# Accumulating the weighted sum of squares of a double RMS norm on VectorE instead of TensorE

## The reference, cut to what matters

```python
def rms_norm(x, g):
    xf = x.astype(jnp.float32)
    y = xf * lax.rsqrt(jnp.mean(xf * xf, axis=-1, keepdims=True) + EPS)
    return (y * g.astype(jnp.float32)).astype(x.dtype)

# end of the first block
    x = x + peer_layer(rms_norm(x, norm_ffn_g), w_peer_q, peer_keys, peer_u, peer_v)
    return rms_norm(x, norm_final_g)
# start of the second block (x is what the first one returned)
        h = rms_norm_2(x, norm_g[l]) * (1.0 + scl[:, None, :]) + shift[:, None, :]
        proj = h @ w_in[l]
```

## Time and profile before

| | |
|---|---|
| median of three runs | 2390.09 us (2389.08 to 2395.07) |
| profiled execution, its own time | 2384.56 us |
| its span, first to last instruction | 2382.8 us |
| TensorE matmul busy over the span | 2057.4 us (86%) |
| VectorE busy | 1554.3 us (65%) |
| ScalarE busy | 479.9 us (20%) |
| GpSimd busy | 835.0 us (35%) |
| mean granted TensorE clock | 0.921 of full speed |

### The profile page before, as it was taken

One profiled execution on the slowest core, in us unless ns is written; L12 is line 12 of the kernel. 1 busy time (PEld: TensorE's weight loads), 2 busy tenths in 40 slices (PEclk: granted clock), 3 DMA queues, 4 the chain that ended last, 5 costly groups with the idle time before them and its releaser, 6 DMA issues. The chain is left out here.

```text
span 2382.8 us, 24401 instructions
## 1 busy us (share of the span) xinstructions
PE 2057.4 (86%) x8044; PEld 1367.7 (57%) x8044; DVE 1554.3 (65%) x3438; ACT 479.9 (20%) x1077; POOL 835.0 (35%) x633
## 2 busy tenths in 40 slices
PE   5998789969798989989889889988866679989977
PEld 4875468748547966555555555555422367724445
DVE  4468746459999956666666666666777676246752
ACT  3344122222212320000000000000000131335541
POOL 3420034423110026655555445454676222300002
PEclk8988589979899989999999999999988789999999
DMA  7976879667473679999999999999999421100012
GB/s 282 347 288 203 300 287 390 237 259 264 169 280 118 212 287 396 404 403 402 402 402 402 403 404 402 402 402 403 402 399 401 188 94 62 53 22 1 1 36 70
DMA packets 203900, 648.09 MB, mean 272 GB/s; under 512 B 19840, under 2 KB 52736, under 8 KB 202496
## 3 DMA queue, kind: packets, MB, share of 16 engines
q1 hardware_dynamic: 118384, 335.60, 37.9%
q0 software_dynamic: 73728, 268.47, 28.6%
q10 hardware_dynamic: 11664, 42.47, 5.2%
HBM read 560.48 MB, written 85.98 MB: 271 GB/s over the span
## 5 line engine op out<-in xcount | busy, mean ns | idle before, releaser
L1591 PE MATMUL ps<-arena 128*128 128x512 f32 x1024 | 519.2, 655 | 144.6 <-DVE arena L1448 92.5
L1459 DVE CUSTOM_DVE_ANT_0 arena<-arena 128x1024 bf16<-128x1024 f32 x256 | 313.3, 1224 | 246.4 <-DMA arena<-u_rows,u_row 132.8
L1580 PE MATMUL ps<-rows_n,arena 128*128 128x256 f32 x2048 | 464.7, 379 | 0.0
L1580 PEld LDWEIGHTS ps<-rows_n,arena 128*128 128x128 f32 x2048 | 387.0, 190 | 96.3 <-issue 50.4
L1591 PEld LDWEIGHTS ps<-arena 128*128 128x128 f32 x1024 | 207.9, 209 | 399.5 <-issue 269.1
L1323 POOL DMA_INDIRECT arena<-u_rows,u_row x256 | 290.7, 1136 | 313.2 <-DMA gates<-arena 168.5
L1323 POOL DMA_INDIRECT arena<-in_v,expert x192 | 209.3, 1090 | 315.9 <-DVE arena L1480 288.2
L1480 DVE SCALAR_TENSOR_TENSOR arena<-arena,wt 128x1024 f32<-128x1024 f32 x192 | 246.1, 1282 | 0.5
L1557 ACT ACTIVATE ge<-dots 128x2 f32<-128x2 f32 x128 | 26.0, 203 | 913.8 <-DVE dots L1459 913.8
L190 DVE STREAM_TRANSPOSE tdst<-tsrc 128x1024 f32<-128x1024 f32 x128 | 154.8, 1228 | 80.9 <-DMA tsrc<-in_u 43.8
L234 POOL TENSOR_TENSOR in_wlo<-in_raw,in_whi 128x1024 fp32r<-128x1024 f32 x45 | 114.2, 2539 | 235.6 <-ACT in_whi L230 235.6
(11 more groups left out here) (390 smaller groups left out, 2925.8 us busy)
## 6 DMA issues: line engine op xcount, KB each, us to landing
tsrc<-in_u SPq DMA_DIRECT2D x128, 512.0 KB, 7.8
u_rows<-tdst SPq DMA_DIRECT2D x128, 512.0 KB, 6.4
arena<-in_u SPq DMA_DIRECT2D x128, 512.0 KB, 10.6
arena<-in_v SPq DMA_DIRECT2D x128, 512.0 KB, 12.1
in_raw<-in_panels ACTq DMA_DIRECT2D x37, 512.0 KB, 3.8
gates<-arena SPq DMA_DIRECT2D x8, 2048.0 KB, 8.7
arena<-gates SPq DMA_DIRECT2D x32, 512.0 KB, 18.8
mg_raw<-in_panels ACTq DMA_DIRECT2D x28, 512.0 KB, 7.1
```

The costliest lines, as they stand in the source:

```text
L1459: nc.vector.tensor_tensor_reduce(out=junk[:, n % 2], in0=u_slot[n % NU], in1=hrows[:, n // NPICK], scale=1.0, scalar=0.0, op0=ALU.mult, op ...
L1580: mm = nc.tensor.matmul(ps[:, j % 2, 0:TD], ud[:, j % RJ, k], rows_n2[:, 0, k], start=k == 0, stop=k == KD - 1)
L1591: mm = nc.tensor.matmul(ps[:, 4 + 2 * t + c], park[:, j % NPK, t * P:(t + 1) * P], vd[:, j % RJ, c * T:(c + 1) * T], start=j == 0, stop=j ...
```

## The change

Bank 1 is no longer summed by TensorE over eight products with weighted matrices. ScalarE squares all eight tiles. VectorE multiplies each squared tile by its gain and adds it to one 128x512 tile `acc` (in the space of `ang`), and TensorE makes one product of `mean1024` with `acc` at the end. TensorE's products fall from sixteen to nine. VectorE loses the eight 128x128 weightings and its four squares, and gets eight operations on 128x512, each of which waits for ScalarE's square and for the one before it. The semaphore `sq_dve` goes.

```diff
-                mean_g = ang[:].rearrange("p a (b e) -> p (a b) e", e=P)
+                acc = ang[:, 0]
@@ block.scalar
-                    for k in range(0, KD, 2):
+                    for k in range(KD):
                         nc.scalar.activation(sq[:, k], xT[:, k], ACT.Square).then_inc(sq_act, 1)
@@ block.tensor
                     for k in range(KD):
-                        pe.wait_ge((sq_act, sq_dve)[k % 2], k // 2 + 1)
+                        pe.wait_ge(sq_act, k + 1)
                         mm = nc.tensor.matmul(ps[:, 0], cst("mean1024"), sq[:, k], start=k == 0, stop=k == KD - 1)
-                        if k == KD - 1:
-                            mm.then_inc(sum_x, 1)
-                        pe.wait_ge(weighted, k + 1)
-                        mm = nc.tensor.matmul(ps[:, 1], mean_g[:, k], sq[:, k], start=k == 0, stop=k == KD - 1)
-                    mm.then_inc(sum_xg, 1)
+                    mm.then_inc(sum_x, 1)
+                    pe.wait_ge(weighted, KD)
+                    nc.tensor.matmul(ps[:, 1], cst("mean1024"), acc, start=True, stop=True).then_inc(sum_xg, 1)
@@ block.vector
                     for k in range(KD):
-                        nc.vector.tensor_scalar(mean_g[:, k], cst("mean1024"), gain_sq[:, k:k + 1], None, ALU.mult).then_inc(weighted, 1)
-                        if k % 2:
-                            nc.vector.tensor_tensor(sq[:, k], xT[:, k], xT[:, k], ALU.mult).then_inc(sq_dve, 1)
+                        v.wait_ge(sq_act, k + 1)
+                        if k == 0:
+                            ins = nc.vector.tensor_scalar(acc, sq[:, k], gain_sq[:, k:k + 1], None, ALU.mult)
+                        else:
+                            v.wait_ge(weighted, k)
+                            ins = nc.vector.scalar_tensor_tensor(out=acc, in0=sq[:, k], scalar=gain_sq[:, k:k + 1], in1=acc,
+                                                                 op0=ALU.mult, op1=ALU.add)
+                        ins.then_inc(weighted, 1)
```

More of the change, by code:

```diff
@@ L1708, in two_norms @@
                 gain_sq = sb(sn, "n3_gain_sq", [P, KD])
-                sq_act, sq_dve, weighted, sum_x, sum_xg, parted, seeded, y_ready, hi_ready, lo_ready, dve = sems(
-                    sn, " ".join("n3_" + s for s in "sq_act sq_dve weighted sum_x sum_xg parted seeded y hi lo dve".split()))
+                sq_act, weighted, sum_x, sum_xg, parted, seeded, y_ready, hi_ready, lo_ready, dve = sems(
+                    sn, " ".join("n3_" + s for s in "sq_act weighted sum_x sum_xg parted seeded y hi lo dve".split()))
                 block = sn.enter_context(nc.Block())
```

## The result

The changed kernel takes 2373.38 us in the median of three runs (2371.19 to 2373.55), against 2390.09 us before; the ratio is 0.9932 with a 95% interval of 0.9908 to 0.9957. Forecast were 2384.1 us and a gain of 6.0. Over ten more runs on another chip the ratio was 0.9955 (0.9933 to 0.9976). The medians of three lie 16.7 us apart, nearly three times the forecast; over the ten runs the gain is 12.9 us by medians and 10.8 us by the ratio (5.7 to 16.0), about twice the forecast.

The account below looks back on a forecast made before the run. It took the norm stage as one path, TensorE's 32 passes then VectorE's tail. Fourteen passes at 0.429 us give 6.0 us, feed, engine contention and clock 0: 2390.09 - 6.0 = 2384.1 us, range 2379.6 to 2389.6.

Parts of the forecast that it names:

- the path and the passes: Norm stage: TensorE's 32 passes, then VectorE's tail, form one path; 14 passes go at 0.429 us each, 6.01 us.
- the pass-by-pass sum: Norm stage: start times of passes 7 to 18 and VectorE's reads, putting L1761 at 1897.84, 6.0 us earlier.
- second rival: Norm stage: GpSimd holds the last addition, the sum becomes TensorE's late input; gain 5.2 or 4.5 us; chance 0.12.
- the clock rises at the same moment: Start of the norm stage: clock rises as before, about 1892.2, so all removed passes belong to the fast part.
- the place where two engines meet: VectorE's last addition (k = 7) against GpSimd's two products from 1892.21: price between 0 and 2.2 us, taken as 0.
- the beat of the additions: VectorE's seven dependent additions in the norm stage: 0.725 us from start to start, the last ending at 1892.93.
- The cover is 3.8 us: Norm stage: VectorE's sum ends at 1892.93, TensorE wants `acc` at 1896.71, so the sum is 3.8 us early.
- I take 0 with ±2 us for their sum: Clock's low time at the start of this burst and later ones: 1.05 us up or down each, 0 ±2 in all.
- against the median the forecast is 2390.09 - 6.0: Whole kernel: the profiled execution's 6.0 us gain is taken off the median of the runs, giving 2384.1 us, -0.25%.
- third rival: Projection, 2008 to 2032: the shift could keep the clock low longer, costing 7 us, kernel 2391.1 us; chance 0.03.
- first rival: Every later burst and dip is re-timed: 2 us either way, 2382.1 or 2386.1 us; chance 0.15 fast, 0.06 slow.

Follow-up runs that it names:

- padded_products: Changed kernel plus seven unread products, one behind each of the first seven, so TensorE again has 32 passes in the stage; 2392.83 us, ratio 0.9992.
- squares_only: Kernel before with all eight squares on ScalarE and VectorE's squares taken out, TensorE keeping its sixteen products; 2393.89 us, ratio 0.9997.
- lows_after_sum: Changed kernel with GpSimd waiting for VectorE's complete weighted sum before the low parts of the first two panels; 2376.84 us, ratio 0.9924.
- filled changed kernel: Changed kernel plus four unread products ahead of each of in2's eight score groups and of the attention's first eight score jobs; 2387.36 us, ratio 0.9992.
- pad_3: Changed kernel plus three unread products behind its first three, 24 passes in the stage; 2385.95 us, ratio 0.9986.
- attn_filled_before: Kernel before plus four unread products ahead of each of the last attention's first three score jobs; 2386.07 us, ratio 0.9986.
- pad_5: Changed kernel plus five unread products behind its first five, 28 passes in the stage; 2377.18 us, ratio 0.9951.

## Why the prediction was wrong, point by point

**Right: the path and the passes.** The 14 passes were on the path, at 0.429 us each in both kernels, and everything behind moved as a whole, with TensorE's idle time ahead of in2 unchanged (14.8 us). padded_products shows that nothing else in the change gives anything in the stage; squares_only, that the squares give nothing.

**The stage, 4.87 in place of 6.01.** Two terms of the pass-by-pass sum were mis-sized. The clock rose about a microsecond later behind the first product than before (5.75 us in place of 4.82; over all thirteen profiles it is 3.5 to 5.8): the last of the sixteen passes started at 1887.09 + 9.97 - 0.59 = 1896.47, 9.38 us behind the first, in place of the 8.92 that the earlier trace rows had given. That is a loss of 0.46. And the sum was the late input, the prediction's second rival, put at 0.12: pass 17 started at 1897.48 in place of 1896.90, 0.58 late, and 0.1 more went since the weights could not be loaded ahead; 0.68 together. 0.46 + 0.68 = 1.14, the difference. lows_after_sum gave the 0.68 back, and the filled changed kernel, with one held addition, did not have it. The assumption that the clock rises at the same moment was wrong by 0.9 us; the range allowed for that.

What failed in the second term is "I take 0" for the price of the place where two engines meet, and in front of it the beat of the additions. The prediction took 0.725 us from the Newton chain. Here it is 0.86 (1887.74 to 1892.02 for five), with 0.75 us busy in place of 0.69; whether the second semaphore or the accumulator makes the difference was not tested. GpSimd also started 4.62 us behind the first product, where it had been 4.85. So two additions, k = 6 and 7, lay behind GpSimd's start and not one. VectorE did get in between GpSimd's two products: k = 6 was held by the first, k = 7 by the second. "The cover is 3.8 us" was a cover against slowness, not against being held for 2.65 us twice. (In the second rival's own sum the addition lasts 0.60 us, 1896.86 to 1897.46; the earlier trace rows have 0.69.)

**The other half: a term set to zero.** The step that failed is the last but one, "I take 0 with ±2 us for their sum", for the clock, and with it the next, "against the median the forecast is 2390.09 - 6.0". Both take the profiled execution for the usual one, and the clock behind the stage for noise about zero. In the profiles the work behind the stage was 5.9 and 2.6 us shorter than before, the larger part in in2 (3.5) and the last norm (1.7) of the first; over the runs the gain exceeds the stage's 4.9 by 8 us by medians and by 6 (1 to 11) by the ratio.

The profiled execution was 5.5 us under the median, and the prediction noted this without asking what those 5.5 us are. The record answers in part. A low start of the attention costs 7.4 us and is seen in two of the eight profiles without filler (squares_only, pad_3) and in none of the five with it. If the filler of attn_filled_before removes it, that kernel's 4.0 us for 2.6 us of work mean that the kernel before loses some 6.6 us there in its usual execution (3 to 9 by the interval). But this is an estimate from medians: of the three profiles without filler and with 32 passes in the stage only that of squares_only shows it, and the part ahead of the stage, which varies by up to 10.7 us, can hide as much. That the changed kernel has the slow start less often was not shown; its ten runs, spread over 17 us, don't fall into two clear groups. The third rival had the mechanism, a low stretch whose length hangs on where a shift puts the work, but knew it only from in2 and let it only lengthen; in that stretch it shortened by 3.5 us in the first profile, and hardly in the second (165.65). The first rival named "every later burst" and a size of 2 us, from onsets alone; stretches within dense work were left out of it, and what they cost is 3.5 and 7.4 us.

So of the 12.9 us, 4.9 are the stage, shown by its rows. That the rest is mainly low-clock time behind it is shown by the windows of the profiles and by pad_3 against pad_5, whose profiles differ by 7.4 us in the attention. That the attention's start has a large part in the gain of the changed kernel itself is argued, not shown: in its profile and in that of before the attention ran at full clock. The extra is not a merit of the change: 24 passes lose nearly all of it and 28 keep it.

**Still open.** In how many executions of each kernel the attention's start is slow was not counted; single runs have no window of it. Why stages of 24 and 32 passes gain so much less than those of 18 and 28 was not settled, nor what makes the stage begin 10.7 us earlier or later. The gain above the stage's own would have to be measured anew after any edit ahead of the attention.

## What to carry to other kernels

Before predicting, ask how the profiled execution stands to the median; where it is off by as much as the effect sought, find the stretch in which executions of the same kernel differ, for the change may move just that. A gain much larger than its stage's rows allow calls for a padded version, with the removed time put back in one engine, and then for one or two amounts in between: if the time does not follow the amount, part of the gain is alignment. Compare profiles from the changed stage on, since what lies ahead of it differs too. An accumulation on VectorE from two SBUF tiles should end before GpSimd starts on SBUF, or GpSimd should wait for it: starting GpSimd 2 us later cost nothing here.

## What the hardware showed unexpectedly

- At the start of the attention the same work took 181.5 or 188.9 us, with the granted clock at 1.00 or at 0.53 for 17 us, from one execution to another.
- With a stage longer by 1.6 us (28 passes instead of 24) the kernel was 8.8 us faster (12.0 and 3.2 under the kernel before).
- Twelve unread bf16 products of 128x512, 2.6 us in all, ahead of the attention's first jobs made the kernel before 4.0 us faster by medians (0.5 to 6.0 by the interval). Whether they do it by keeping the clock up no profile shows: that of before had it up there without them.
- With the same instructions ahead of it, the stage began between 1885.4 and 1896.1 us in thirteen profiled executions.
- VectorE's additions with two SBUF operands were held in turn by each of two back-to-back GpSimd products (2.65 us in place of 0.75, twice), and GpSimd's second product was held in between as well: its pair took 5.17 us in place of 4.65. Where GpSimd started 0.5 us later, only one addition was held.
